# A three-layer float32 forward pass on one core: in-projection columns reordered, index queries by halves, scores by pairs of heads, key rope on GpSimd

## What is computed

```
h = x @ w_in                                   # 1024 -> 648
c_q, k, v, k_idx, w_idx = split(h)             # 256, 128, 128, 128, 8 columns
c_q = rms_norm(c_q, g_cq)
q, q_idx = c_q @ w_uq, c_q @ w_iq              # 16 heads of 64; 8 heads of 128
k_idx = layer_norm(k_idx, g_ik, b_ik)
q, k, q_idx, k_idx = rope(each)                # first 16 (q, k) or 32 (index) of a head
score = sum over heads of w_idx * relu(q_idx . k_idx), causal
attend, with q, k, v, to the 64 keys of highest score
```

## Time and profile before

| | |
|---|---|
| median of three runs | 996.75 us |
| profiled execution | 988.9 us, span 987.2 us |
| busy PE / DVE / ACT / POOL | 944.6 / 606.8 / 464.2 / 138.3 us |
| chain that ended last | PE 84%, DVE 9%, ACT 3%, DMA 2%, issue 1%, POOL 1% |
| loaded from HBM | 160.93 MB |

### The profile page before, as it was taken

The page is one execution under the profiler, slowest core; times in us unless marked ns, Lnnn a source line. Parts: engine busy times, 40 slices in busy tenths (PEclk is TensorE's granted clock), DMA queues, the critical chain, the costliest instruction groups (busy, mean ns, idle before and its releaser), DMA issues.

```text
span 987.2 us, 11869 instructions
## 1 busy us (share of the span) xinstructions
PE 944.6 (96%) x4717; PEld 779.5 (79%) x4717; DVE 606.8 (61%) x960; ACT 464.2 (47%) x616; POOL 138.3 (14%) x115
## 2 busy tenths in 40 slices
PE   6779999999999998999999999999999999999996
PEld 5657788888887787998788888877787778888885
DVE  4674676464648756978755464585323567767775
ACT  4565344252433453254443433345566465556562
POOL 3163200000001810001100000001174110101010
PEclk9999999999999999999999999999999999999999
DMA  8891356556547653224765655467433355555531
GB/s 281 189 165 34 120 191 199 184 185 199 173 154 228 231 175 108 88 83 128 247 200 173 199 182 187 154 212 256 152 132 123 128 169 190 175 180 187 186 129 42
DMA packets 103510, 165.89 MB, mean 168 GB/s; under 512 B 3931, under 2 KB 72570, under 8 KB 103456
## 3 DMA queue, kind: packets, MB, share of 16 engines
q1 hardware_dynamic: 99968, 152.61, 47.0%
q0 software_dynamic: 3488, 12.53, 5.7%
HBM read 160.93 MB, written 4.19 MB: 167 GB/s over the span
## 4 chain that ended last, share of the span: by engine, by line
PE 84%; DVE 9%; ACT 3%; DMA 2%; issue 1%; POOL 1%; DVEq 0%; POOLq 0%; ACTq 0%
PE PG L1758 12%; PE PG L1760 12%; PE PG L1759 12%; PE PA L1758 12%; PE PA L1760 11%; PE PA L1759 11%; PE PA L2161 2%; DVE wlo L586 1%; PE PG L1890 1%; ACT whi L577 1%; PE TB L2292 1%; PE TB L1907 1%; PE TB L2002 1%; DVE xlo L1070 1%; DVE stats L1132 1%
## 5 line engine op out<-in xcount | busy, mean ns | idle before, releaser
L586 DVE TENSOR_TENSOR wlo<-raw,whi 128x2048 fp32r<-128x2048 f32 (+1 forms) x129 | 300.5, 2345 | 80.5 <-ACT whi L577 80.4
L577 ACT ACTIVATE whi<-raw 128x2048 fp32r<-128x2048 f32 (+1 forms) x142 | 268.5, 1907 | 52.6 <-PE PA L1760 19.5
L1758 PE MATMUL PG<-whi,xlo 128*128 128x512 f32 x560 | 223.2, 399 | 4.0 <-DVE wlo L1288 2.9
L1760 PE MATMUL PG<-whi,xhi 128*128 128x512 f32 x560 | 219.1, 391 | 0.0
L1759 PE MATMUL PG<-wlo,xhi 128*128 128x512 f32 x560 | 218.7, 391 | 0.0
L1758 PE MATMUL PA<-whi,xlo 128*128 128x512 f32 (+1 forms) x344 | 137.5, 400 | 10.1 <-DVE xlo L1070 5.2
L1760 PE MATMUL PA<-whi,xhi 128*128 128x512 f32 (+1 forms) x344 | 132.7, 386 | 0.0
L1759 PE MATMUL PA<-wlo,xhi 128*128 128x512 f32 (+1 forms) x344 | 132.4, 385 | 0.0
L1758 PEld LDWEIGHTS PG<-whi,xlo 128*128 128x128 f32 x560 | 105.8, 189 | 26.0 <-DVE wlo L1288 3.3
L1760 PEld LDWEIGHTS PG<-whi,xhi 128*128 128x128 f32 x560 | 105.5, 188 | 22.6
L1759 PEld LDWEIGHTS PG<-wlo,xhi 128*128 128x128 f32 x560 | 105.8, 189 | 20.6
(11 more groups left out here) (264 smaller groups left out, 1084.2 us busy)
## 6 DMA issues: line engine op xcount, KB each, us to landing
raw<-in_ffn_w_gate SPq DMA_DIRECT2D x44, 512.0 KB, 4.0
raw<-in_ffn_w_up SPq DMA_DIRECT2D x44, 512.0 KB, 5.0
raw<-in_ffn_w_down SPq DMA_DIRECT2D x22, 1024.0 KB, 4.8
raw<-in_w_up SPq DMA_DIRECT2D x44, 512.0 KB, 4.8
raw<-in_hgrn_w_in SPq DMA_DIRECT2D x16, 1024.0 KB, 5.3
raw<-in_w_qkv SPq DMA_DIRECT2D x12, 1024.0 KB, 5.2
raw<-in_w_down SPq DMA_DIRECT2D x11, 1024.0 KB, 4.9
raw<-in_att_w_o SPq DMA_DIRECT2D x4, 1024.0 KB, 5.7
```

The costliest lines, as they stand in the source:

```text
L577: nc.scalar.activation(whi[:, g, 0:n_], raw[:, s, 0:n_], ACT.Copy).then_inc(S("w_hi"), 1)
L586: nc.vector.tensor_tensor(wlo[:, s, 0:n_], raw[:, s, 0:n_], whi[:, g, 0:n_].bitcast(F32), ALU.subtract).then_inc(S("w_lo"), 1)
L1758: mm(dst, xl[:, k, rows], whi[:, g, cols], start=first, stop=False)
L1760: return mm(dst, xh[:, k, rows], whi[:, g, cols], start=False, stop=last_)
```

## The change

The weight columns of units 0 and 1 are now 0 to 255 and 392 to 647 (latent query, all but 8 of the value's columns, index key, index weights), loaded in two DMAs per half with 1 KB rows; unit 2 is columns 256 to 391 (key, first 8 of the value). In `pin` the value starts at 248, over the end of the latent query, so its 8 columns are copied after `cqn`; the key is at 512.

Index key norm moves ahead of the latent query's normalising, with one inverse square root call for both. On PE the latent query's turn comes after 6 of the 8 tiles of unit 2, the bias goes to PG. Index queries are made in two column halves, into PA[0:2] and PA[2:4], with the index key's turn between them; ACT copies the first half, ACT and DVE a row tile each of the second; each half has its own rope. Scores go by pairs of heads, with the turns of later pairs between. `hi(6)` comes after the relus. The first query half goes to PG, the second to PA[0:2]. The key's rope and doubling go to POOL, behind all accumulations; its turn stands after the queries, with five more warming matmuls ahead of it and four after the first logits. POOL's wait for `w_loaded1` goes to 32, with the doubled DMAs.

```diff
@@ weight_units
-    a = up(w_in, 0)
-    a.append([(0, 8, IN_COLS - 512, w_in.rearrange(...)[:, :, 512:IN_COLS])])
+    a = [[v[:, 4 * j:4 * j + 4, c:c + EARLY] for c in (0, SKIP)] for j in range(2)]
+    a.append([(0, 8, SKIP - EARLY, v[:, :, EARLY:SKIP])])
@@ sync
-                    sp.dma_start(dst, view[:, 2 * g:2 * g + 2, :]).then_inc(S(landed_), 16)
+                    for s, view in enumerate(units[u]):
+                        sp.dma_start(dst[:, :, s, :], view[:, 2 * g:2 * g + 2, :]).then_inc(S(landed_), 16)
@@ gpsimd
-            power(C_CQ)
-            power(C_KEY)
+            power(C_IN)
             load_gb(0)
...
             pool.wait_ge(S("trig"), 1)
+            pool.wait_ge(S("k_in"), 2)
+            pool.wait_ge(S("iacc"), 2 * HI)
+            link(rope(pool, link, pin[:, :, C_K:C_K + P].rearrange("p r (g c) -> p r g c", g=2), 2, ROT, 0))
+            for r in range(RT):
+                for c in range(2):
+                    ins = pool.tensor_copy(kd[:, r, :, c, :],
+                                           pin[:, r, C_K:C_K + P].rearrange("p (g c) -> p g c", g=2))
+            ins.then_inc(S("kd"), 1)
@@ scalar
             hi(2)
+            hi(3)
...
-            hi(3)
             hi(4)
             turned(ev["cq"])
             ac.activation(flat(xhi[:, 0:2, :]), TB[:, ev["cq"] % 2, :], ACT.Copy).then_inc(S("x_hi"), 1)
+            act.wait_ge(S("cqn"), 1)
+            full(2)
+            ac.activation(pin[:, :, C_K:C_K + P], PA[:, 2:4, 0:P], ACT.Copy).then_inc(S("k_in"), 1)
+            ac.activation(pin[:, :, C_V:EARLY], PA[:, 2:4, P:SKIP - EARLY], ACT.Copy).then_inc(S("k_in"), 1)
             hi(5)
-            full(U_IQ)
-            ac.activation(qi[:, 0, :], flat(PA[:, 0:2, :]), ACT.Copy).then_inc(S("qi_a"), 1)
+            act.wait_ge(S("iq_first"), 1)
+            ac.activation(qi[:, :, 0:HALF], PA[:, 0:2, :], ACT.Copy).then_inc(S("qi_a"), 1)
...
+            ac.activation(kiT, TB[:, e % 2, 0:T], ACT.Copy).then_inc(bank_free(e), 1)
+            full(U_IQ)
+            ac.activation(qi[:, 1, HALF:D], PA[:, 3, :], ACT.Copy).then_inc(S("qi_a"), 1)
-            copy_turned("qi", qiT)
-            hi(6)
+            index_turned(0)
+            index_turned(1)
             for hd in range(HI):
...
                 ac.activation(relu[:, hd % 2, :], PA[:, hd % 4, 0:384], ACT.Relu).then_inc(S("relu"), 1)
+                if hd in (1, 3):
+                    index_turned(2 + hd // 2)
+            hi(6)
+            act.wait_ge(S("ssq"), RT)
+            ac.activation(sq[:, 0, 0:1], sq[:, 0, 0:1], ACT.Exp, scale=0.0)
...
+            e = ev["kk"]
+            turned(e)
+            ac.activation(flat(kT), TB[:, e % 2, :], ACT.Copy).then_inc(bank_free(e), 1)
             copy_turned("q", qT)
@@ vector (index-key moments now here, ahead of the latent query's variance)
             lo(2)
+            lo(3)
+            vec.wait_ge(S("pin"), 1)
...
-            ve_.tensor_copy(qi[:, 1, :], flat(PA[:, 2:4, :])).then_inc(S("qi_b"), 1)
-            rope(ve_, link, qi.rearrange("p r (g c) -> p r g c", g=HI), HI, ROTI, ROT).then_inc(S("qi_r"), 1)
             lo(4)
+            vec.wait_ge(S("ki_r"), 1)
+            for f in range(2):
+                if f:
+                    full(U_IQ)
+                    ve_.tensor_copy(qi[:, 0, HALF:D], PA[:, 2, :]).then_inc(S("qi_b"), 1)
...
+                vec.wait_ge(S("qi_a"), f + 1)
+                q_half = qi[:, :, f * HALF:(f + 1) * HALF].rearrange("p r (g c) -> p r g c", g=HI // 2)
+                rope(ve_, link, q_half, HI // 2, ROTI, ROT).then_inc(S("qi_r"), 1)
@@ tensor
+            later_columns(range(6))
             e = ev["cq"]
...
+            later_columns(range(6, KT)).then_inc(S("w_used"), 1)
+            mm(PG[0:HQ, 0, 0:T], relT[0:BUCKETS, :], hot[0:BUCKETS, :], start=True, stop=True).then_inc(S("reldist"), 1)
...
-            down(U_IQ, 0, True, True)
+            halves(U_IQ, 0, lower).then_inc(S("iq_first"), 1)
...
+            pe.wait_ge(S("k_in"), 2)
+            halves(U_IQ, 1, upper).then_inc(S("w_used"), 1)
...
+            pe.wait_ge(S("qi_r"), 1)
+            turn_rows("qi", qi, events=range(2))
+            parts_ready(ev["ki"])
+            scores(0)
+            for g in range(1, 4):
+                if g < 3:
+                    pe.wait_ge(S("qi_r"), 2)
+                    turn_rows("qi", qi, events=(g + 1,))
+                scores(g)
+            pe.wait_ge(S("relv"), 1)
+            pe.wait_ge(S("w_lo"), U_UQ + 1)
+            halves(U_UQ, 0, lambda r: PG[:, r, :]).then_inc(S("first_q"), 1)
+            pe.wait_ge(S("relu"), HI)
+            halves(U_UQ, 1, lower).then_inc(S("w_used"), 1)
+            keep_warm(WARM)
+            e = ev["kk"]
+            pe.wait_ge(S("kd"), 1)
...
             def first_logits():
+                keep_warm(4)
                 turn_rows("q", qr, lambda g: pe.wait_ge(S("q_r"), 2), range(2, 4))
                 keep_warm(WARM)
```

More of the change, by code:

```diff
@@ L32 @@
 IN_COLS = 648
-C_K, C_V, C_KI, C_WI = 256, 384, 512, 640
+SKIP, EARLY = 392, 256
+C_V, C_KI, C_WI, C_K = 248, 376, 504, 512
 FF = 2816
@@ L559, in build @@
         for u in range(U_ALL + RING):
-            two = any(u - up_unit(U, i) in (0, 1) for U in (U_F0, U_F1, U_F2) for i in range(NFF))
+            two = u < 2 or any(u - up_unit(U, i) in (0, 1) for U in (U_F0, U_F1, U_F2) for i in range(NFF))
             total[u % RING] += 32 if two else 16
@@ L1312, in _ @@
             lo(2)
+            lo(3)
+            vec.wait_ge(S("pin"), 1)
+            for r in range(RT):
+                ins = ve_.bn_stats(stats[:, r, 0, :], pin[:, r, C_KI:C_WI])
+            link(ins)
+            for r in range(RT):
+                ins = ve_.bn_aggr(mv[:, 2 + r, :], stats[:, r, 0, :])
+            link(ins)
+            ve_.tensor_scalar(ve[:, 2:4], mv[:, 2:4, 1], LN_EPS, None, ALU.add)
             vec.wait_ge(S("ssq"), RT)
@@ L1329, in _ @@
             ins.then_inc(S("cqn"), 1)
[L1330 to L1349, removed]
             for r in range(RT):
@@ L2031, in _, with later_columns @@
             last.then_inc(S("t_full"), 1)
-            pe.wait_ge(S("w_lo"), 3)
[L2034 to L2039, removed]
+            def later_columns(ks):
+                for k in ks:
+                    for r in range(RT):
+                        last = products(PA[:, 2 + r, 0:136], k, r, U_IN + 2, slice(k * 136, (k + 1) * 136), k == 0,
+                                        k == KT - 1)
+                return last
+            pe.wait_ge(S("w_lo"), 3)
+            later_columns(range(6))
             e = ev["cq"]
@@ L2048, in _, with halves @@
             last.then_inc(S("t_full"), 1)
-            parts_ready(e)
-            pe.wait_ge(S("relv"), 1)
-            down(U_IQ, 0, True, True)
-            e = ev["ki"]
+            later_columns(range(6, KT)).then_inc(S("w_used"), 1)
+            parts_ready(ev["c0"])
+            pe.wait_ge(S("pin"), 1)
+            mm(PG[0:HQ, 0, 0:T], relT[0:BUCKETS, :], hot[0:BUCKETS, :], start=True, stop=True).then_inc(S("reldist"), 1)
+            def halves(u, f, bank):
+                for r in range(RT):
+                    for t in range(2):
+                        last = products(bank(r), t, r, u, slice(t * D + f * HALF, t * D + (f + 1) * HALF),
+                                        t == 0, t == 1)
+                return last
@@ new lines, in _ @@
+            lower, upper = lambda r: PA[:, r, :], lambda r: PA[:, 2 + r, :]
+            parts_ready(e)
+            pe.wait_ge(S("w_lo"), U_IQ + 1)
+            halves(U_IQ, 0, lower).then_inc(S("iq_first"), 1)
+            e = ev["ki"]
+            pe.wait_ge(S("ki_r"), 1)
+            t_bank(e)
+            for r in range(RT):
+                last = nc.tensor.transpose(TB[:, e % 2, r * P:(r + 1) * P], pin[:, r, C_KI:C_WI], ident[:, :])
+            last.then_inc(S("t_full"), 1)
+            pe.wait_ge(S("k_in"), 2)
@@ new lines, in _, with scores @@
+            halves(U_IQ, 1, upper).then_inc(S("w_used"), 1)
+            def scores(g):
+                parts_ready(ev["qi"] + g)
+                for hd in (2 * g, 2 * g + 1):
+                    if hd >= 4:
+                        pe.wait_ge(S("relu"), hd - 3)
+                    mm(PA[:, hd % 4, 0:128], qiT[:, hd, 0:P], kiT[:, 0:P], start=True, stop=True)
+                    mm(PA[:, hd % 4, 128:384], qiT[:, hd, P:T], kiT, start=True, stop=True).then_inc(S("iscore"), 1)
+            pe.wait_ge(S("qi_r"), 1)
@@ L2054, in _, with keep_warm @@
+            halves(U_UQ, 1, lower).then_inc(S("w_used"), 1)
+            def keep_warm(n_):
+                for _ in range(n_):
+                    mm(PA[:, 3, :], xhi[:, 4, 0:P], flat(xhi[:, 4:6, :]), start=True, stop=True)
+            keep_warm(WARM)
+            e = ev["kk"]
             pe.wait_ge(S("kd"), 1)
```

78 lines of the change are left out of this document (26 added, 52 removed).

## The result

The kernel after took 982.61 us (median of 981.80, 982.40, 982.81, 984.05) against 995.78 (994.36, 994.81, 996.75, 997.92): ratio 0.987, 95% interval 0.984 to 0.989. It is 13.2 us faster. Predicted were 990.0 and, for the range, 986.5 to 994.5: the sign was right and the size outside the range. The profiled execution of after took 981.8 us (span 979.9), that of before 988.9 (987.2): 7.1 apart, against a sum of 6.8. So the two profiles say what the sum said, and the medians say twice as much. The rest of this document is about both.

A forecast was written before the change was run, and what follows sets the result against it. With PE busy 178.16 of 180 us from 112 to 292, attention's start was taken to count. Terms 1.2 + 6.4 - 0.4 - 0.4 = 6.8 us, so 996.75 - 6.8 = 990.0; range 986.5 to 994.5.

The forecast's parts named there:

- Reference: Whole kernel: subtract the 6.8 us sum from the profiled 988.9 (982.1) and from the median 996.75 (990.0).
- slower: Rival, in-projection: 1 KB rows leave gaps, PE stays at 1.2 GHz, all 86 matmuls cost 17.2 us, giving 1007; 5%.
- PE to the end of the index queries: PE from 24.32 us: earlier latent query turn, index matmuls done at 37.0 instead of 38.2; gain 1.2 us.
- From there to the first accumulation: Index matmuls' end to DVE's first accumulation: 2.5 us instead of 9.0, so at 39.5; gain 6.4 us (5.5 to 7).
- Scoring by pairs: Index scores: turns and copies for heads 4 to 7 between scores delay relus; loss 0.4 us (0 to 1.5).
- Second logits: First attention: four more warming matmuls and two query turns stand before the second logits; loss 0.4 us (0 to 0.8).
- Start-up: Loads of units 0 and 1 in 1 KB rows: no gain possible, taken as 0, range 0 to +0.5 us.
- Key on POOL: Key rope and doubling on POOL behind all accumulations: ready at 49.8, costing nothing while under about 4.6 us.
- DMAs that move: Bias scratch and output-weight loads issued earlier: fourth unit lands near 63.5, wanted at 66.8, so covered.
- late weights: Rival: scratch write catches the third output-weight unit, up to 6.4 us lost, giving 992 to 996.3; 13%.
- short of the sum: Rival: slower ropes, ping-pong at its 1.5 us, or POOL's key work near 10 us; typically 991 to 994; 13%.
- hidden: Rival: gain reappears as an equal wait behind attention; time within 2 us of 996.75; 3%.

The follow-up runs named there:

- e5: Kernel before with its three long PE waits filled by 10, 8 and 5 unused warming matmuls: 991.64 us, ratio 0.997 to before.
- e8: Kernel after with the latent query's turn behind all eight tiles of the 136 columns, as before: 988.28 us, ratio 0.992 to before.
- e3: Kernel before with one edit, ACT's conversion of unit 6 moved behind the eight relus: 993.31 us, ratio 0.998 to before.
- e6: Kernel after with ACT's conversion of unit 6 back ahead of the relus: 984.0 us, ratio 0.989 to before.
- e7: Kernel after with all four turns and copies of the index queries ahead of the first score: 991.63 us, ratio 0.994 to before.
- e11: Kernel after with the key's rope and doubling back on DVE, ahead of the accumulations: 984.51 us, ratio 0.990 to before.
- e2: Kernel after, unchanged, run and profiled again: 984.25 us over 8 runs, ratio 0.990 to before.
- e1: Kernel before, unchanged, run and profiled again: 993.99 us over 10 runs, ratio 0.998; its profiled execution took 998.05 us.
- e4: Kernel after without its nine added warming matmuls, five before the key's turn and four behind the first logits: 986.15 us, ratio 0.990 to before.

## Why the prediction was wrong in size and right in its steps

**The step that failed is "Reference".** It set the profile of before, 988.9, beside the median, 996.75, saw 7.9 us between them, and moved the sum across them unchanged: 996.75 - 6.8 = 990.0. That took the 7.9 us for something that both kernels have. It wasn't: the profiled execution was one of the few (4 of 65 since) in which PE keeps full clock nearly throughout, and the 6.5 us above that level are half-speed stretches. After shortened or warmed PE's waits of 2.92, 2.36 and 1.30 us in that stretch (now 0.83 at most between 40 and 74 us), and reaches 0.996 or more in 14 of 16. With each kernel at 0.998 the prediction's other line stands: 982.1 was its figure on the profile's own time, 981.8 was measured, and 982.0 is the median of after at that clock. The missed term is 5.9 us. It is most of the 7.4 between 990.0 and the measured 982.6; another 1.0 is that the median of before came out at 995.8 instead of 996.75, and 0.5 that the schedule brought 7.3 instead of 6.8. That the two kernels differ in clock is shown by the table; that the filled waits raise it, by e5; how much of the 5.9 each wait is worth is not shown.

The clock was in the prediction, but only as the rival "slower", for the in-projection, and only against the change. Two things in front of me spoke for the other side: the gap of 7.9 us, more than twice the 3.6 us that the three runs spread over, and the long waits of PE themselves, which the change removes.

The terms of the sum, one by one. Their misses of 0.1 to 0.4 us have both signs and partly cancel:
- *PE to the end of the index queries*, 1.2: measured 1.4. The turn of the latent query behind 36 matmuls is 1.08 of it (e8).
- *From there to the first accumulation*, 6.4: 6.2 (9.0 us before, 2.8 now against 2.5 predicted). The rope of 128 elements was taken as 1.35 and measured 1.4; the second is hidden as said. Of these 6.2, e3 and e6 bear 0.9 and 1.1 for the conversion; halves and pairs against whole blocks were not undone by themselves.
- *Scoring by pairs*, loss 0.4: 0.03. ACT's relus for two heads start 1.75 us apart (38.90, 40.65, 42.40), where DVE accumulates two in 1.70, so DVE is held up by hundredths of a microsecond only. As against all turns first, the pairs bring about 1.6 us (e7).
- *Second logits*, loss 0.4: 0.5 (1.53 us of DVE's wait, 1.03 before).
- *Start-up*, 0: right within the spread. PE runs 0.43 a matmul until 13.2 (13.5 before); the copy is at 23.86 (23.93), and 24.16 against 24.07 in the means above.
- *Key on POOL*, free: right (e11). Six operations of 32 elements took 0.24 to 0.25 each as estimated; the four copies took 1.00 together where 1.7 was put. Ready at 48.9, predicted 49.8.
- *DMAs that move*, free: right, by less than thought. The third unit landed at 35.4, before the write, issued at 31.9, could hold it. The fourth landed at 65.5, not 63.5. The write ended 4.3 us earlier than before (67.3 against 71.6), but the load did not move with it: issued 1.5 us earlier, it took the same 28.7 us. That leaves 1.0 us of margin, 0.0 in e2, against 3.3 as put, so "late weights" was closer than its 13% says. By the packet-by-packet rule quoted there (the Trainium skill, DMA: Bandwidth & Descriptors, Queues, rings and completion order) the load should share with the write from its issue on. The trace agrees with the rule in the second half of the 28.7 us (243 packets against 242) and not in the first, in which no packet of the load moved. What holds the load back there stays open.

The rivals "late weights", "short of the sum" and "hidden" show no trace. "Slower" named the right engine and had the wrong sign. Its price was wrong as well: the in-projection has 48 matmuls of 512 columns, not 96, and nine of them ran at half speed, so the 39 others could cost 7.8 us at most, not 17.2, and that is less than the 9.8 the rival needed. And that PE kept its pace behind 1.41 us of idle time was read from one execution: in the profile of e5 the clock falls behind that same wait.

**What stays open:** which of the waits matters how much, and what makes one execution of a program drop and the next not. Filling the three waits (e5) brings between 0.7 and 5.4 us of the 5.9, and drops in attention's later stretches (77 to 94), all behind the same wait of 1.1 us, come in e1, e3, e4 and e8 with no edit there.

## What to carry to other kernels

Before a profile is used as the reference of a sum, compare its time with the timed runs: if they differ by more than the runs spread, find what differs (here the mean granted clock, 0.998 against 0.987 to 0.991), and ask of the change whether it shortens or lengthens PE's waits. Time an order of work by positions relative to an instruction that stands the same in both kernels; that showed steps of 0.1 to 1 us that ten runs could not. And an early hand-over is worth having twice: for the chain it shortens, and for the idle gap of PE that it closes.

## What the runs showed of the hardware

- PE's clock falls to 1.2 GHz in the middle of a kernel that has kept it busy for hundreds of microseconds, and in different places in different executions. Beside e1 and e6, e2 shows it at 662 us, behind a wait of 2.02 us for DVE, in its timeline of PE:

```profile
662.63 1.72 PE L1767 MATMUL TB<-ident,work 128*128 128x128 f32 x8 [2.02 <-DVE work L1229]
...
665.00 0.63 PE L1778 MATMUL PA<-whi,xhi 128*128 128x512 f32 x1
```

  The profile of the same program after has the same work there, behind a wait of 2.05 us, at PEclk 1.00. So a wait of that length needn't bring a drop, and the profile of before has 2.92 and 2.36 and none. But no drop came without a wait of 1.08 us or more close ahead of it, in 22.
- Each 0.001 of mean clock costs about 0.8 us of 990 (989.3 at 0.998, about 998 at 0.987).
- Issued beside the 3 MB write of the bias scratch, a 1 MB load takes 28.7 to 29.7 us in the profiles of before and after, about half of them standing still; issued 1.6 us before the write, 5.1 in after's profile.
- POOL's operations on 32 elements a partition are 0.21 us apart, on 128 elements 0.42 (46.41 to 46.62 and so on, 49.42 to 49.84): four times the work for twice the time.
